# Eight named loads of one activation table set around the root stages, and thin products of 512 columns, in a fp32 two-layer block

## The reference

```python
def rmsnorm(x, g): return x * rsqrt(mean(x * x, -1) + EPS) * g

# layer 1: a Mamba-2 scan and a short convolution side by side, then a feed-forward part
h = rmsnorm(x, mix_pre_g) * (1 + sc1) + sh1          # sc, sh, gt: c_act @ ada_w + ada_b
proj = h @ w_in                                      # 1024 -> z, xbc, dt, sc_b, sc_c, sc_h, gates
y_ssd = grouped_rmsnorm(ssd(silu(conv(xbc)), softplus(dt)) * silu(z)) @ w_ssd_out
mix = (g_ssd * y_ssd + g_sc * short_conv(...) @ w_sc_out) @ w_o
x = x + gt1 * rmsnorm(mix, mix_post_g)
h = rmsnorm(x, ffn_pre_g) * (1 + sc2) + sh2
f = (silu(u_gate) * u_val) @ w_down                  # u = conv(h @ w_up), 2 x 2816 wide
x = x + gt2 * rmsnorm(f, ffn_post_g)
# layer 2: NSA attention (compressed, selected, window) and MLA attention side by side
h = rms_norm(x, attn_norm) * (1 + scale_a) + shift_a
q, k, v, latents = split(h @ w_in_2)                 # each head of q and k normed, rope
kc = rms_norm(compress(rope(k)), kc_norm)
q_b, kv_b = rms_norm(cq) @ w_uq, rms_norm(ckv) @ w_ukv
x = x + gate_a * ((g_a * o_a + g_b * o_b) @ w_o)
x = x + gate_f * ffn_2(rms_norm(x, ffn_norm) * (1 + scale_f) + shift_f)
```

## Time and profile before

| | |
|---|---|
| median of the runs | 1059.93 us |
| span of the profiled execution | 1056.5 us |
| time of that execution | no own value is given; the median is 3.4 us above its span |
| VectorE busy | 556.2 us, 53% |
| ACT busy | 634.4 us, 60% |
| GpSimd busy | 689.8 us, 65% |
| table loads on ACT | 33, 1283 ns each |

### The profile page before, as it was taken

The page is one execution under the profiler, slowest core; times in us unless marked ns, Lnnn a source line. Parts: engine busy times, 40 slices in busy tenths (PEclk is TensorE's granted clock), DMA queues, the critical chain, the costliest instruction groups (busy, mean ns, idle before and its releaser), DMA issues.

```text
span 1056.5 us, 23232 instructions
## 1 busy us (share of the span) xinstructions
PE 1025.1 (97%) x8537; PEld 966.4 (91%) x8537; DVE 556.2 (53%) x1165; ACT 634.4 (60%) x1133; POOL 689.8 (65%) x306
## 2 busy tenths in 40 slices
PE   7999999999999989999999899999989999999998
PEld 5999999988799979999999799998667699999998
DVE  2577625579874435565522542296566735444400
ACT  4555764477774576666645656744566557666642
POOL 2598899811269855988799287790031075988795
PEclk9999999999999999999999999999999999999999
DMA  9988888655547863777687289865201043665563
GB/s 380 383 306 282 273 307 298 235 191 187 174 146 259 282 236 105 273 235 248 204 279 268 80 283 360 330 239 191 99 21 60 1 140 122 217 193 189 168 217 111
DMA packets 62616, 226.43 MB, mean 214 GB/s; under 512 B 6960, under 2 KB 8272, under 8 KB 61264
## 3 DMA queue, kind: packets, MB, share of 16 engines
q1 hardware_dynamic: 61344, 221.23, 60.5%
q10 hardware_dynamic: 1200, 4.23, 1.4%
HBM read 224.35 MB, written 1.08 MB: 213 GB/s over the span
## 4 chain that ended last, share of the span: by engine, by line
PE 75%; issue 9%; POOL 9%; DVE 3%; ACT 3%; DMA 1%; POOLq 0%; ACTq 0%; DVEq 0%; SPq 0%
PE psL L553 68%; POOL WL L505 8%; PE psO L553 3%; PE psS L553 2%; PE psL L1092 1%; DMA ring<-wts 1%; ACT psL L1685 0%; ACT WH L1155 0%; ACT R L1273 0%; PE psS L1036 0%; ACT L1146 0%; DVE sm L2288 0%; PE psS L1063 0%; PE psS L966 0%; DVE CT L2052 0%
## 5 line engine op out<-in xcount | busy, mean ns | idle before, releaser
L505 POOL TENSOR_TENSOR WL<-ring,WH 128x1024 fp32r<-128x1024 f32 (+1 forms) x282 | 670.4, 2399 | 239.8 <-ACT WH L1155 186.7
L553 PE MATMUL psL<-HR,WH 128*128 128x256 f32 (+1 forms) x3096 | 513.5, 278 | 1.8 <-DVE HR L1796 0.9
L553 PEld LDWEIGHTS psL<-HR,WH 128*128 128x128 f32 (+1 forms) x3096 | 452.6, 187 | 7.5 <-issue 4.8
L553 PE MATMUL psL<-HR,WL 128*128 128x256 f32 x1536 | 396.2, 276 | 0.0
L1155 ACT ACTIVATE WH<-ring 128x1024 fp32r<-128x1024 f32 (+1 forms) x210 | 216.5, 1042 | 107.8 <-PE psL L553 71.9
L553 PEld LDWEIGHTS psL<-HR,WL 128*128 128x128 f32 x1536 | 275.2, 188 | 0.0
L553 PE MATMUL psL<-RR,WH 128*128 128x256 f32 x1356 | 205.2, 277 | 2.4 <-DVE RR L1981 1.2
L553 PEld LDWEIGHTS psL<-RR,WH 128*128 128x128 f32 x1356 | 185.5, 187 | 3.8 <-issue 2.8
L553 PE MATMUL psL<-RR,WL 128*128 128x256 f32 x672 | 145.0, 277 | 0.3 <-POOL WL L505 0.3
L2080 DVE SCALAR_TENSOR_TENSOR CT<-psL,par,CT 128x254 f32<-128x254 f32 (+1 forms) x176 | 80.9, 480 | 107.1 <-ACT CT L1463 102.0
L1454 ACT ACTIVATE WH<-ring 128x1024 fp32r<-128x1024 f32 (+1 forms) x88 | 92.9, 1058 | 71.4 <-PE psL L553 68.0
(11 more groups left out here) (274 smaller groups left out, 1122.8 us busy)
## 6 DMA issues: line engine op xcount, KB each, us to landing
ring<-wts SPq DMA_DIRECT2D x285, 512.0 KB, 4.2
adaring<-ada_w SPq DMA_DIRECT2D x80, 512.0 KB, 4.8
R<-ada_w SPq DMA_DIRECT2D x8, 1024.0 KB, 16.2
ring<-wts SPq DMA_DIRECT2D x16, 384.0 KB, 3.8
R<-cum_dram ACTq DMA_DIRECT2D x8, 512.0 KB, 4.1
R<-wts SPq DMA_DIRECT2D x8, 512.0 KB, 6.4
ring<-wts SPq DMA_DIRECT2D x8, 288.0 KB, 2.8
adaring<-wts SPq DMA_DIRECT2D x4, 512.0 KB, 5.2
```

Source lines behind the costliest of these rows:

```text
L505: nc.gpsimd.tensor_tensor(WL[:, k, 0:n], ring[:, k, 0:n], WH[:, k, 0:n].bitcast(F32), SUB).then_inc(lo_done, 1)
L553: return nc.tensor.matmul(out, lhsT, rhs, start=start, stop=stop)
```

## The change

A helper, `roots_table()`, loads the table set that holds both Ln and Exp by its name. It stands at eight places: behind the SiLU of the start, behind the first 24 units of `in1`, ahead of the `CD` copy, at the start of `scale_and_square` for `o1` and for `down1`, behind `turned_mix` in `feat2`, in `latent_roots`, and at the last unit but one pair of `ukv`. Two named loads of SiLU's set stand before loops of `in1`. `preload()` and its calls go. The root of kc is taken by Ln and Exp where it was Sqrt on ACT and a reciprocal on VectorE. In `o1` and `down1` the last `feed` (the copy of the next stage's fourth chunk) stands behind the root's Exp, where it stood ahead of its Ln. The thin products are three of 32 x 512 where they were six of 32 x 256; their moving operand is a pair of regions of the operand.

```diff
+        def pair_of(buf, one, other):
+            step = abs(other - one)
+            def at(k):
+                first = buf[:, min(one, other) + k * T:min(one, other) + (k + 1) * T]
+                return bass.AP(first.tensor, first.offset, [list(first.ap[0]), [step, 2], [1, T]])
+            return at
...
             def thin_products(u, weights, rhs):
-                for _ in range(6):
-                    mm(psL[0:32, u % 4, T:2 * T], weights, rhs, True, True)
+                for _ in range(3):
+                    mm(psL[0:32, u % 4, :], weights, rhs, True, True)
...
-            linear8("in1", SLOTS, 24 - SLOTS, h_hi, h_lo, late=SLOTS, thin=True)
+            linear8("in1", SLOTS, 24 - SLOTS, h_hi, h_lo, late=SLOTS, thin=pair_of(HR, 0, 2048))
...
+            def roots_table():
+                nc.scalar.preload_act_table_set("natural_log_exp_and_others")
...
             A(csil[:, :], pv("c_2"), ACT.Silu).then_inc(csil_ready, 1)
+            roots_table()
             act.wait_ge(x_in, 16)
...
             units("in1", 0, 24, begin_xbc)
             act.wait_ge(par2_in, 16)
+            roots_table()
...
+            nc.scalar.preload_act_table(ACT.Silu)
             units("in1", 24, 4, z_bank)
...
             units("in1", 48, 16, None)
+            roots_table()
             n = SCRATCH["dt_turn"]
             act.wait_ge(s_done, n + 1)
             A(CD[:, :, :].rearrange("p a b -> p (a b)"), psS[:, n % 2, 0:128], ACT.Copy).then_inc(s_free[n % 2], 1)
...
-            def preload():
-                st.link(A(sm[:, 94:95], eps_col[:, :], ACT.Ln))
...
                 act.wait_ge(lead_ready, 1)
+                roots_table()
                 for m in range(8):
...
-                    feed(u)
-                    if m == 6:
-                        preload()
+                    if m < 7:
+                        feed(u)
...
             def square_x(base, sq_free_after):
-                preload()
                 act.wait_ge(s_done, sq_free_after + 1)
...
             scale_and_square("o1", MIX, lead[:, 8:16], 0, SQ_O1)
             stat_root("stat_o1", D, RS[:, 0, :])
+            feed(PLAN.at["o1"][1] + 7)
             square_x(0, SCRATCH["stat_o1"])
...
             stat_root("stat_down1", D, RS[:, 0, :])
+            feed(PLAN.at["down1"][1] + 7)
             square_x(8, SCRATCH["stat_down1"])
...
                     turned_mix()
+                    roots_table()
                     act.wait_ge(tok_sq, 24)
...
             def latent_roots():
+                roots_table()
...
-            A(sm[0:30, 60:61], sm[0:30, 60:61], ACT.Sqrt, scale=1.0 / HD, bias=eps_col[0:30, :]).then_inc(kc_rs, 1)
+            st.link(A(sm[0:30, 60:61], sm[0:30, 60:61], ACT.Ln, scale=1.0 / HD, bias=eps_col[0:30, :]))
+            A(sm[0:30, 60:61], sm[0:30, 60:61], ACT.Exp, scale=-0.5).then_inc(kc_rs, 1)
...
                 square_o2(m)
-                if m == 6:
-                    preload()
...
-            st.link(V.reciprocal(sm[0:30, 60:61], sm[0:30, 60:61]))
```

More of the change, by code:

```diff
@@ L600, in thin_products, with late_unit @@
             def thin_products(u, weights, rhs):
-                for _ in range(6):
-                    mm(psL[0:32, u % 4, T:2 * T], weights, rhs, True, True)
-            def late_unit(u, q, nchunks, hi, lo, operand=None, thin=False):
+                for _ in range(3):
+                    mm(psL[0:32, u % 4, :], weights, rhs, True, True)
+            def late_unit(u, q, nchunks, hi, lo, operand=None, thin=None):
                 bank_wait(u)
@@ L612, in late_unit @@
                     if thin and c == 0:
-                        thin_products(u, WH[:, s, 0:32], hi(0))
+                        thin_products(u, WH[:, s, 0:32], thin(0))
                     for b in range(8):
@@ L643, in together, with linear8 @@
                             last.then_inc(lin_done, 1)
-            def linear8(name, first, count, hi, lo, operand=None, joint=0, late=0, thin=False):
+            def linear8(name, first, count, hi, lo, operand=None, joint=0, late=0, thin=None):
                 q0, u0 = PLAN.q(name) + first, PLAN.at[name][1] + first
@@ L653, in linear8 @@
                 for c in range(joint, done):
-                    late_unit(u0 + c, q0 + c, 1, hi, lo, thin=thin and c == joint)
+                    late_unit(u0 + c, q0 + c, 1, hi, lo, thin=thin if c == joint else None)
                 rounds = (count - done) // SLOTS
@@ L831, in _ @@
                 late_unit(PLAN.at["ssd_out"][1] + m, PLAN.q("ssd_out") + 2 * m, 2, lambda k: ZH[:, k, :], lambda k: ZL[:, k, :],
-                          operand=lambda k: pe.wait_ge(zl_ready, k // 4 + 1) if m == 0 and k % 4 == 0 else None, thin=m == 1)
-            linear8("o1", 0, 8, lambda k: MH[:, k, :], lambda k: ML[:, k, :], from_count(ml_ready, 0), 2, 6, True)
+                          operand=lambda k: pe.wait_ge(zl_ready, k // 4 + 1) if m == 0 and k % 4 == 0 else None, thin=pair_of(RR, 4096, 18432) if m == 1 else None)
+            linear8("o1", 0, 8, lambda k: MH[:, k, :], lambda k: ML[:, k, :], from_count(ml_ready, 0), 2, 6,
+                    pair_of(RR, 2048, 16384))
             u0 = PLAN.at["up1"][1]
@@ L843, in _ @@
             fill(u0, 4)
-            linear8("up1", 0, 44, h_hi, h_lo, from_count(h_ready, 8), 3, 5, True)
+            linear8("up1", 0, 44, h_hi, h_lo, from_count(h_ready, 8), 3, 5, pair_of(HR, 0, 2048))
             for m in range(8):
@@ L880, in _ @@
                     if c == 1 and part == 0:
-                        thin_products(u0 + 2 * c, HH[:, 0, 0:32], WH[:, s, 0:256])
+                        thin_products(u0 + 2 * c, HH[:, 0, 0:32], WH[:, s, 0:512])
                     for t in range(2):
@@ L905, in _ @@
                 nc.tensor.transpose(out[:, 0:88], KRGT[:, t * P:(t + 1) * P], pv("ident", 0, 88)[0:88, :]).then_inc(s_done, 1)
-            linear8("feat2", 1, 8, h_hi, h_lo, late=4, thin=True)
+            linear8("feat2", 1, 8, h_hi, h_lo, late=4, thin=pair_of(HR, 0, 2048))
             pe.wait_ge(sq_ready, 38)
@@ L1129, in _ @@
             fill(u0, 4)
-            linear8("up2", 0, 44, h_hi, h_lo, from_count(h_ready, 24), 3, 5, True)
+            linear8("up2", 0, 44, h_hi, h_lo, from_count(h_ready, 24), 3, 5, pair_of(HR, 0, 2048))
             for m in range(8):
```

## The result

The changed kernel takes 1066.61 us (median of four runs, 1061.81 to 1068.49) against 1059.65 for the kernel before, run beside it: a ratio of 1.0067, 95% interval 1.0046 to 1.0089. It is slower by 7 us, where I forecast 4.2 us faster, and it lies outside the range of 1051.0 to 1058.8. The profiled execution took 1061.81 us with a span of 1060.0. So 1.8 us lie outside the span, and not the 3.4 I took from the median: by the same 1.8 the profile of before was itself an execution about 1.6 us better than its median, and that of after is the best of its four. The two profiles are therefore only 3.5 us apart, half of the 7.

What follows compares the result with a forecast made beforehand. The prediction took TensorE's matmuls as the bound, busy 1025.1 us of a 1056.5 us span. Its terms summed to −4.2 us, from 1059.9 to 1055.7 us, with a range of 1051.0 to 1058.8.

Steps and rivals of the forecast that it cites:

- Thin products: At seven places, three of 512 columns stream the same columns as six of 256: −0.1 us, at most +4.8.
- Root behind o1: First root gains 0 as GpSimd's subtraction holds VectorE's adds; second loses a load, −1.3 us; low clock charged +0.7.
- Root behind down1: First root +0.6 us as held adds outweigh the load gone; second gives 1.28 back; together −0.7.
- From in1 to the scan: Named load ahead of the CD copy delays it and the copies the scan's scores wait for: +1.1 us.
- third rival: Low clock spreads from longer TensorE gaps at o1 and down1 into later units: +3.1 us, 1063.0; chance 0.05.
- Start of down1: Named load ahead of two chunk copies makes GpSimd start later, delaying the remainder TensorE needs: +0.4 us.
- Group norm: Load of line 1301 gone, so ACT's chunk copies come 1.28 us earlier and TensorE's units wait less: −1.1 us.
- Latents: Load of line 1575 gone at the latent roots, so TensorE keeps its lead over GpSimd's subtractions longer: −1.0 us.
- Start: Load between Ln and Exp at the kernel's start gone, gain limited by TensorE's idle products: −0.6 us.
- o2: Root behind o2: loads delaying squares and standing between Ln and Exp are gone, nothing moved behind: −1.6 us.
- First rival: GpSimd's subtraction doesn't hold VectorE's adds at o1 and down1: −9.1 us, 1050.8; chance 0.14.
- Second: Rival: ACT's gains at start, group norm and latents come to nothing: −1.5 us, 1058.4, not measurable; chance 0.17.

Runs made afterwards that it cites:

- e1: The changed kernel with the old thin products, six of 32 x 256, put back: 1060.55 us, ratio 1.0014.
- e2: The kernel before with only the thin products changed, to three of 32 x 512: 1068.72 us, ratio 1.0109.
- e6: e5 with two named loads moved: in1-to-scan's behind the XTOK copies, down1's behind its first unit: 1049.19 us, ratio 0.9918.
- e10: e6 with the changed kernel's three thin products of 32 x 512: 1057.93 us, ratio 0.9981.
- e12: The kernel before with only the last chunk's copy of o1 and down1 moved behind the root's Exp: 1065.83 us, ratio 1.0067.
- e5: e1 with the last chunk's copy of o1 and down1 moved from behind the first root's Exp to behind make_h: 1052.06 us, ratio 0.9942.
- e3: The kernel before with three thin products of 32 x 256 in place of six: 1056.59 us, ratio 0.9976.
- e8: The kernel before without any thin products: 1059.50 us, ratio 1.0023.
- e11: The kernel before with only the last chunk's copy of o1 and down1 moved behind make_h: 1059.51 us, ratio 1.0011.
- x1: e6 with the wide products' columns, operand regions and bank, cut into six thin products of 32 x 256: 1048.91 us, ratio 0.9911.
- e9: e6 with three thin products of 32 x 256 in place of six: 1050.98 us, ratio 0.9921.
- e4: The kernel before with six thin products of 32 x 512, twice the columns: 1068.36 us, ratio 1.0117.

## Why the prediction was wrong

Two steps of the prediction failed, each enough to miss: the price of the thin products, and the gain of 4.1 on ACT. With the thin products at no cost (e1) the time is still 1060.55, above the range and no gain.

**Thin products, forecast −0.1, measured about +6** (e1 beside the changed kernel), +10 to +12 alone (e2, by the medians and by the ratio), +7 to +9 on e6 (e10). This is the step that made a clear loss of it. I wrote that six of 256 and three of 512 "stream the same columns, so I take −0.1", with +4.8 as the upper end for a dearer form, and asked only what the products themselves cost. That part was right: three wide ones take 0.69 us up to the next matmul, six narrow ones 0.68. What they fail to do to the matmuls behind them is the price: they leave units at 2.83 us where 2.72 follows the old ones. The profile of before showed both paces: slow ahead of the thin products of ssd_out, o1, up1 and tok2, fast behind them. I had the rows of eight matmuls at 1.10 and at 1.07 us in the timeline and took the difference for noise. The signs that I had named to tell right from wrong came out right almost one and all (no load in the roots, an add of 2.83, low windows at o1, wide products 0.23 apart), since none of them looked at the units behind the thin products. An instruction whose result nobody reads has a purpose, and I didn't ask for it.

**Root behind o1, forecast −0.6 in all.** The mechanism was right in each part: the second add is held 2.15 us (I had 2.4), TensorE has a gap of 2.33 us (2.5), and the clock falls behind it. In the profile of after this root is −0.5. The size of the clock was off: I charged 0.7 once. In e1 and e12 it stays at 0.50 for six windows and not three, and the root comes out at +0.5 (e1) and +3.8 (e12, which keeps the old loads). That the profile of after comes so near the forecast is luck: it has the short stretch.

**Root behind down1, forecast −0.7**: 0.0 in after, +0.8 in e1. The add takes 2.84 there too. I took the clock there as paid already, and it cost more: in e1 six windows at 0.50 (587 to 593), where the kernel before has two and two at 0.65.

**From in1 to the scan, forecast +1.1, measured +1.7** in after, +1.0 in e1, and 1.9 between e5 and e6. The load was right; the low clock behind TensorE's wait of 1.8 us was missing in the term. The third rival had named the spread of the low clock, and gave it 0.05: it fell in the scan and at both roots (down1's was low before), though up1's first units, where I looked for it, ran at 1.00.

**Start of down1, forecast +0.4**: +0.7; the profile shows a wait of 0.4 us for the remainder, and the other 0.3 stays open. e6 takes all of it back.

**Group norm, forecast −1.1**: −0.9 in after, in e1 and in e6 alike, and nothing in e12, which has the old loads. Right.

**Latents, forecast −1.0**: −1.2 in after, and the number deceives. In e3, e8 and e11, which have no table load moved, the same units gain 1.2, and in x1, which has the change's loads, they lose 0.7. The loss in the profile of before was that execution's and not the load's. I can't assign any gain to the change here.

**Start, forecast −0.6**: −0.6 in after, 0.0 in e1, −0.6 in e5, and +0.6 in e12, whose start is that of before. It is within what executions differ by.

**o2, forecast −1.6, measured −0.6** in after and e6. The loads are gone and the root comes earlier, and then the last chunk's subtraction (872.91 to 875.26) holds make_h, for 0.64 of the 1.0 us that are missing. It is the mechanism of o1, and I left it out where nothing had been moved.

**First rival** (VectorE is not held): wrong, with 2.83 us for an add of 0.69. **Second** (only the path of the roots gains): its three terms went −0.9, nothing, and undecided. Drain behind a load: no row shows it; at the group norm and at o2, ACT goes on at once.

So the work on ACT was worth −4.1 in the forecast and is +1.5 (−0.6 to +3.5) in e1: with the copy elsewhere (e5) it is −6.1, and with the two loads elsewhere (e6) −8.7, all by the ratios. The table set was a good idea with two bad places, and one bad place for a copy.

## What to carry to other kernels

Ask of every instruction that looks useless what comes after it: count the matmuls per microsecond in stretches where TensorE is never idle, before and behind it. A copy that is moved off the critical chain releases its followers elsewhere; look where they will run, above all GpSimd's, when VectorE's chain is the critical one. A gap of TensorE can cost its length and then the half clock behind it, here about as much again (2.15 and 2.1 us at o1 in e1).

## What the runs showed of the hardware

- TensorE has two steady paces for the same matmuls at the same granted clock of 1.00: 0.113 and 0.118 us for 256 columns (179 and 172 in 20 us). The slow one lasted through all of up1 and down1 in e8. What sets it in the engine stays open. Thin products ahead of a unit can turn it from slow to fast: six of 32 x 256 did at 17 places of 17 (before, e1, e5, e6, e11, e12, x1), three at 5 of 9 (e3, e9), three of 512 columns at none of 11 (after, e2, e10), six of them at 1 of 4 (e4).
- Runs of one kernel, with nothing changed, differ by 8 to 12 us (e8, e9, e10), and one long stage at the slow pace is worth nearly 7 of that (up1 with down1 in the profiles of e8 and e9, up2 with down2 in that of e10).
- An operation of VectorE with two inputs in SBUF that meets GpSimd's subtraction stands still until that ends: 2.83 for 0.69 us (after, e1, e12). GpSimd's takes 2.75 us and not 2.35 when it starts under an operation of VectorE (after, e12).
- The granted clock fell to 0.50 behind a gap of TensorE of 1.8 us (scan, after), and at the end of or within one of 2.3 us (o1, after and e1). It stayed there for some three windows of 1 us in after and six in e1. In e5, with gaps of at most 0.97 us at o1, it stayed at 1.00 there.
